# A two-layer hybrid decoder step: the opening of layer 0 rearranged (norm factors as rows, fewer and longer weight sums, waits by row group)

## The chip, the cores and the metric

The kernel runs on one core of one Trainium2 chip. The metric is the device time of one execution in microseconds: 2112.86 us, the median of three runs (2112.59 to 2115.5). The core has five engines that run side by side and wait for each other by semaphores: TensorE (PE in the profile) for matrix products and transposes, VectorE (DVE), ScalarE (ACT), GpSimd (POOL), and SyncE (SP), which only issues transfers. TensorE's clock has two levels, 1.2 and 2.4 GHz; the profile shows it as the granted clock, 0.50 or 1.00.

## The reference

Two layers work on a prompt of 2048 tokens and on a sample of 64 tokens (8 sequences of 8), with width 1024. Each layer does this:

```python
u = rms_norm(x, norm_gain)                  # x / rms(x) * gain, the gain has 1024 values
proj = u @ w_in                             # 1024 x 3592, in float32
# three head groups read the same proj
h_m = sigmoid(mo) * mlstm(mq, mk, mv, i_pre, f_pre, C0, n0, m0)
h_r = retention(rope(rq), rope(rk), rv, S0)
h_a = window_attention(aq, ak, av, k_buf, v_buf, pos0, sinks, rel_table)
mix = concat(head_norm(h_m) * silu(mz), head_norm(h_r) * silu(rz), h_a * silu(az))
x = x + mix @ w_out
```

A last RMSNorm follows. The states, the normalisers and the last window of keys and values are outputs as well. What matters here is the projection: the gain is multiplied into the rows of the weights, and the weights are used in a form that has to be made on the chip first.

## The kernel before

The prompt is processed in chunks of 128 tokens, 16 a layer. The projection's weights lie in eight blocks of columns; in the order in which they are made ready they are gates (264 columns), rqk, akv (256), rvz, aq, az, mqk, mvo (512 each where no number stands). A block has eight row groups of 128 rows, which is the contraction split into eight. A product of one chunk with one block is 24 matmuls, three a row group, because both operands are kept as two float16 parts: high by high, high by low, low by high (`pair_products`, L547 to L552).

In the first unit of each layer, a block goes through these steps:

1. *Load.* GpSimd issues the load of the block's float32 weights (`load_raw`, L398). The first three are issued at once, each later one when the maximum of an earlier block is known; the last waits for the low parts of the third block.
2. *Size.* ScalarE sums the absolute values of row groups 0 to 5, one sum a row group, by an activation with an accumulator (`abs_sum` L447, `block_sum` L455), alternating between two scratch rows, so that a sum waits only for the one before the previous. VectorE takes the absolute maximum of row groups 6 and 7, multiplies all eight numbers by the size of the gain, and takes the largest (`block_max`, L469 to L477).
3. *Maximum over partitions.* TensorE turns the column of 128 maxima into a row (`top_turn`, L504), VectorE reduces it to one number (`top_of_all`, L508), and TensorE spreads that to all partitions (`top_spread`, L512).
4. *Scale.* VectorE derives a power of two from it and the scales of the eight row groups (`block_scale`, L519 to L529).
5. *Parts.* ScalarE writes the high part, one instruction a row group (`block_hi`, L537), and VectorE the low part behind it (`block_lo`, L544).
6. *Products.* TensorE multiplies the first chunk with the block (`first_block`, L989), once all eight low parts are there, and the sample with the block (`sample_block`, L1002). ScalarE empties both (`evac_first` L1383, `evac_sample` L1406); SyncE stores the sample's result (`keep_sample`, L774), and ScalarE's copy of sample block p waits for the store of block p - 2.

The order of instructions on each engine is written out by hand: `start_act` and `start_dve` hold the opening, `prompt_pe`, `prompt_act` and `prompt_dve` the first unit, `prompt_sp` SyncE's part. Between the blocks stand other steps of the first unit: the copy and the store of a Toeplitz table of the attention bias (1600 KB, sent from 8 partitions, L717, `store_toeplitz`), read back by `load_bias` (L723 to L727); the gate rows (L1886 to L1908); GpSimd's rope (L2302 to L2311).

In the opening, SyncE issues, in this order, the first prompt rows, the identity, small constants, the norm factors (L379) and the sample's rows (L706). VectorE does the prompt's norm, the size of the gain (L467), all of the sample's norm (L1720 to L1729), then the gates block's maximum. ScalarE does the sample's root before the gates block's sums. After the first unit, a loop does the other chunks; there the weights are ready, and each block is one product of 24 matmuls.

Layer 1's blocks go through the same functions during the output projection of layer 0.

## Time and profile before

| | |
|---|---|
| time, median of 3 runs | 2112.86 us (2112.59 to 2115.5) |
| the profiled execution, its own time | 2116.62 us |
| its span in the profile | 2114.80 us |
| TensorE busy | 2016.7 us, 95% of the span |
| VectorE / ScalarE / GpSimd busy | 1661.0 / 890.0 / 330.4 us |
| mean granted clock of TensorE | 0.979 |

The profile is one execution, with times from the start of its span. A row of the timeline or of the groups names the line of the kernel, the engine, the operation, and what is written from what. In square brackets stands how long the engine had stood before it, and what ended that.

### The profile page before, as it was taken

Reading aid. Unit: us, or ns where it says so; the run is one execution under the profiler, and the core shown is the slowest. Engines: PE = TensorE matmul, PEld = TensorE weight load, DVE = VectorE, ACT = ScalarE, POOL = GpSimd, SP = SyncE. Lnnn points to the kernel's source line nnn. Section 1 sums busy time; section 2 is a strip of 40 time slices with the busy share of each in tenths; the row PEclk is TensorE's granted clock in tenths of the full one; section 3 lists DMA queues with packets and bytes.
Section 4 is the critical chain, followed back from the end, with each engine's and each line's share of the span. In section 5 each row is a group of like instructions: output and inputs, shape, how many; then the busy total and the mean of one; then the engine's idle time right before and its main releaser. Section 6 shows DMA issues by size and latency. Waiting matters only on the chain.

```text
span 2114.8 us, 36272 instructions
## 1 busy us (share of the span) xinstructions
PE 2016.7 (95%) x12814; PEld 1133.3 (54%) x12814; DVE 1661.0 (79%) x3966; ACT 890.0 (42%) x2334; POOL 330.4 (16%) x320
## 2 busy tenths in 40 slices
PE   3799999999999999999979999999999999998997
PEld 2465555555555555444455555555555555554453
DVE  5778887888888888675465888888888888887856
ACT  5854444445444445231255444444444444462100
POOL 1101121111111112120010111111111111111200
PEclk9899999999999999999989999999999999999999
DMA  7411121111121114785522111211111211257642
GB/s 247 125 40 42 42 50 43 51 41 41 41 61 41 41 42 131 173 248 155 185 105 64 42 42 42 61 42 41 41 41 44 50 41 51 63 157 177 160 119 90
DMA packets 258349, 175.09 MB, mean 83 GB/s; under 512 B 217880, under 2 KB 231897, under 8 KB 258077
## 3 DMA queue, kind: packets, MB, share of 16 engines
q1 hardware_dynamic: 242244, 142.14, 26.4%
q0 software_dynamic: 7424, 29.43, 3.9%
q10 hardware_dynamic: 8568, 2.18, 0.5%
q8 instruction: 52, 0.85, 0.2%
q14 instruction: 61, 0.49, 0.1%
HBM read 85.29 MB, written 42.29 MB: 60 GB/s over the span
## 4 chain that ended last, share of the span: by engine, by line
PE 62%; issue 18%; DVE 12%; POOL 3%; ACT 3%; DMA 2%; POOLq 0%; SPq 0%; DVEq 0%; ACTq 0%
PE J L551 35%; PE J L1263 12%; PE W L954 2%; DVE W L544 2%; PE W L965 1%; PE J L1002 1%; PE W L1038 1%; ACT junk L450 1%; DMA sc_xr<-in_x_sample 1%; POOL ST L2274 1%; PE W L1068 1%; PE W L1056 1%; PE W L1027 1%; POOL ge L2269 1%; POOL ST L2265 1%
## 5 line engine op out<-in xcount | busy, mean ns | idle before, releaser
L551 PE MATMUL J<-W,x_mix 128*128 128x512 f16 (+2 forms) x3072 | 612.6, 357 | 5.9 <-ACT PB L1383 3.9
L551 PE MATMUL J<-W,uT_mix 128*128 128x512 f16 (+2 forms) x3072 | 612.9, 357 | 2.7 <-DVE W L544 2.6
L551 PEld LDWEIGHTS J<-W,x_mix 128*128 128x128 f16 x3072 | 300.0, 99 | 278.9 <-issue 14.9
L551 PEld LDWEIGHTS J<-W,uT_mix 128*128 128x128 f16 x3072 | 299.7, 99 | 275.8 <-issue 13.9
L1383 ACT ACTIVATE PB<-J,out_scale 128x512 f32<-128x512 f32 (+2 forms) x256 | 154.3, 603 | 294.0 <-PE J L551 286.2
L1353 ACT ACTIVATE ST<-ST,small 128x1024 f16<-128x1024 f32 x32 | 36.7, 1148 | 198.6 <-DVE small L1844 198.6
L1263 PE MATMUL J<-W,EM_qkR_mix 128*128 128x512 f16 x480 | 115.3, 379 | 0.0
L2274 POOL TENSOR_TENSOR ST<-ST,ge 128x512 f32<-128x512 f32 x32 | 67.8, 2117 | 220.5 <-DVE ST L1828 220.5
L1263 PE MATMUL J<-W,x_mix 128*128 128x512 f16 x400 | 99.6, 389 | 0.0
L1263 PE MATMUL J<-W,uT_mix 128*128 128x512 f16 x400 | 99.4, 388 | 0.0
L1347 ACT ACTIVATE sc_xr<-sc_xr,small 128x128 f32<-128x128 f32 x256 | 98.6, 388 | 0.0
L1747 DVE TENSOR_TENSOR ge<-ge,gr 128x512 f32<-128x512 f32 (+1 forms) x96 | 57.4, 598 | 35.3 <-ACT gr L1319 35.3
L2269 POOL TENSOR_TENSOR ge<-ge,PB 128x512 f32<-128x512 f32 x32 | 40.6, 1270 | 272.7 <-DVE ge L1749 272.7
L2265 POOL TENSOR_TENSOR ST<-HH,ge 128x512 f32<-128x512 f32 x32 | 41.4, 1293 | 250.9 <-DVE HH L1784 250.9
L1263 PEld LDWEIGHTS J<-W,EM_qkR_mix 128*128 128x128 f16 x480 | 47.0, 98 | 55.6
L1819 DVE TENSOR_TENSOR ST<-ST,k 128x2048 f16<-128x2048 f16 x62 | 73.1, 1220 | 2.0 <-DMA ST<-ST 2.0
L954 PE MATMUL W<-kTA,qTA_part 64*128 64x256 f32 (+1 forms) x512 | 62.3, 382 | 9.2 <-DVE SR L1766 9.2
L1263 PEld LDWEIGHTS J<-W,x_mix 128*128 128x128 f16 x400 | 40.1, 100 | 48.6 <-issue 5.1
L1263 PEld LDWEIGHTS J<-W,uT_mix 128*128 128x128 f16 x400 | 40.0, 100 | 48.2 <-issue 4.7
L1623 ACT ACTIVATE small_o<-small_o 128x1 f32<-128x1 f32 (+1 forms) x17 | 3.4, 202 | 147.7 <-DVE small_o L2184 131.3
L2285 POOL TENSOR_TENSOR ge<-ge,PB 128x256 f32<-128x256 f32 x32 | 23.8, 743 | 254.9 <-DVE ge L1749 254.9
L1749 DVE SCALAR_TENSOR_TENSOR ge<-ge,gr 128x512 f32<-128x512 f32 (+1 forms) x96 | 59.8, 623 | 3.3
(467 smaller groups left out, 3523.9 us busy)
## 6 DMA issues: line engine op xcount, KB each, us to landing
W<-in_w_in POOLq DMA_DIRECT2D x8, 2048.0 KB, 12.3
mix_d<-ST SPq DMA_DIRECT2D x32, 512.0 KB, 2.6
sc_xr<-in_x_prompt SPq DMA_DIRECT2D x20, 512.0 KB, 4.1
sc_xr<-x SPq DMA_DIRECT2D x20, 512.0 KB, 3.8
ST<-in_w_in POOLq DMA_DIRECT2D x4, 2048.0 KB, 12.5
W<-in_w_out SPq DMA_DIRECT2D x4, 2048.0 KB, 8.3
PB<-in_x_prompt SPq DMA_DIRECT2D x6, 512.0 KB, 3.7
x<-PB SPq DMA_DIRECT2D x6, 512.0 KB, 3.6
```

Source lines behind the costliest of these rows:

```text
L544: nc.vector.scalar_tensor_tensor(pair[b][:, k, 1, :], raw(layer, b)[:, k, :], gs[:, j, k:k + 1], pair[b][:, k, 0, :], ALU.mult, ALU.subtra ...
L551: mm = nc.tensor.matmul(out, stationary(k, a), moving[:, k, b, :], start=(k == 0 and n == 0), stop=(k == KT - 1 and n == 2))
L954: mm = MM(bank[:, t * 256 + lo:t * 256 + 256], qTA[64 * kv:64 * kv + 64, t, :], kTA[64 * kv:64 * kv + 64, lo:256], start=True, stop=True)
L1263: mm = nc.tensor.matmul(J[n], of_tile[:, s, k, :], w[:, cols], start=(k == 0 and i == 0), stop=(k == KT - 1 and i == 2))
L1347: op = af(sc[:, h, :], sc[:, h, :], ACT.Exp, bias=mx[:, h:h + 1], accum_out=rs[:, h:h + 1])
L1383: return af(dst, src, ACT.Copy, scale=scale)
L1747: V.tensor_tensor(y, y, y0, ALU.mult).then_inc(E["gate_inverses"], 1)
L1749: V.scalar_tensor_tensor(y, y, 2.0, y0, ALU.subtract, ALU.mult, reverse0=True).then_inc(E["gate_inverses"], 1)
L1819: op = V.tensor_tensor(pT_both[s], pT_both[1], kept, ALU.mult)
L2265: G.tensor_tensor(mixmr, HH, ge[:, 256:768], ALU.mult).then_inc(E["mixmr_ready"], 1)
L2269: G.tensor_tensor(ge[:, 768:1280], ge[:, 768:1280], PB[:, AZ:IN_COLS], ALU.mult).then_inc(E["gates_a"], 1)
L2274: G.tensor_tensor(mixa, mixa, ge[:, 768:1280], ALU.mult).then_inc(E["mixa_ready"], 1)
```

## The change

- The norm factors are laid out as rows in memory: the array of one layer is 128 x 8 instead of 1024, so that each partition's eight factors lie together, and one plain load brings them.
- SyncE issues the sample's rows first, then the factors, then the small constants.
- The size of a block: in layer 0, ScalarE sums three row groups by one instruction, two sums a block (`abs_sum_wide`), each waiting for the one before; their scratch space is the attention bias, whose load therefore moves from after the fourth block to after the seventh and waits for all of layer 0's sums. VectorE takes one maximum over row groups 6 and 7 and multiplies the largest number by the largest factor of the partition (`gtop`) instead of each by its own. `block_max` is split; the part behind the sums is `block_top`.
- ScalarE does the gates block's sums before the sample's root. The sample's norm is split in three (`sample_size`, `sample_scale`, `sample_rows`), and VectorE does the gates block's maximum between the first two and its scale before the third.
- TensorE waits for the low parts row group by row group in the first unit's products. In layer 0, VectorE takes the maximum of the next block but one after two row groups of low parts for blocks 1 to 3, instead of after all eight.

```diff
         def load_gain(eng, layer):
-            eng.dma_start(norm_g[:], A["norm_gain"][layer].rearrange("(k p) -> p k", p=P),
-                          allow_slow_non_contiguous=True).then_inc(gain_loaded, 16)
+            eng.dma_start(norm_g[:], A["norm_gain"][layer]).then_inc(gain_loaded, 16)
...
+        def abs_sum_wide(act, out, rows):
+
+            wait(act, C["sum_ready"], sums[0])
+            unread = bias[:].rearrange("p h c -> p (h c)").bitcast(BF16)[:, 0:rows.shape[1] * rows.shape[2]]
+            nc.scalar.activation(unread.rearrange("p (k n) -> p k n", k=rows.shape[1]), rows, ACT.Abs, accum_out=out
+                                 ).then_inc(C["sum_ready"], 1)
+            sums[0] += 1
...
-            for k in range(SUM_KS):
-                abs_sum(act, wmax[:, j, k:k + 1], raw(layer, b)[:, k, :])
+            for i in range(SUM_GROUPS[layer]):
+                if layer == 0:
+                    abs_sum_wide(act, wmax[:, j, SUM_KS - 2 + i:SUM_KS - 1 + i], raw(layer, b)[:, 3 * i:3 * i + 3, :])
+                else:
+                    abs_sum(act, wmax[:, j, i:i + 1], raw(layer, b)[:, i, :])
...
             c_prep.step(V.scalar_tensor_tensor(gabs[:], norm_g[:], -1.0, norm_g[:], ALU.mult, ALU.max))
+            c_prep.step(V.tensor_reduce(gtop[:], gabs[:], AX.X, ALU.max))
...
-            st(V.tensor_reduce(wmax[:, j, SUM_KS:KT], raw(layer, b)[:, SUM_KS:KT, :], AX.X, ALU.max,
-                               apply_absolute_value=True))
-            dve.wait_ge(C["sum_ready"], LAYER_SUMS * layer + SUM_KS * (j + 1))
-            st(V.tensor_tensor(wmax[:, j, :], wmax[:, j, :], gabs[:], ALU.mult))
-            V.tensor_reduce(wtop[:, j:j + 1], wmax[:, j, :], AX.X, ALU.max).then_inc(C["max_ready"], 1)
+            st(V.tensor_reduce(wmax[:, j, SUM_KS:SUM_KS + 1], raw(layer, b)[:, SUM_KS:KT, :].rearrange("p k n -> p (k n)"),
+                               AX.X, ALU.max, apply_absolute_value=True))
+
+        def block_top(dve, layer, j):
+            V, st = nc.vector, c_prep.step
+            dve.wait_ge(C["sum_ready"], sums_before(layer, j + 1))
+            first = SUM_KS - SUM_GROUPS[layer]
+            st(V.tensor_reduce(wmax[:, j, SUM_KS + 1:KT], wmax[:, j, first:SUM_KS + 1], AX.X, ALU.max))
+            V.tensor_scalar(wtop[:, j:j + 1], wmax[:, j, SUM_KS + 1:KT], gtop[:], None, ALU.mult
+                            ).then_inc(C["max_ready"], 1)
...
             sp.dma_start(ident, A["c128"][:, 0:P]).then_inc(ident_loaded, 16)
+            sp.dma_start(xs, A["x_sample"].rearrange("b t d -> (b t) d")).then_inc(S["x"], 16)
+            load_gain(sp, 0)
             sp.dma_start(k4[:], A["c4"]).then_inc(ident_loaded, 16)
-            load_gain(sp, 0)
-            sp.dma_start(xs, A["x_sample"].rearrange("b t d -> (b t) d")).then_inc(S["x"], 16)
...
-                if layer == 0 and p == 3:
+                if layer == 0 and p == 6:
+                    sp.wait_ge(C["sum_ready"], sums_before(layer, NBLK))
                     load_bias(sp)
...
-                pe.wait_ge(C["lo"], KT * (NBLK * layer + p + 1))
-                pair_products(J[bank][:, 0:BLOCK[b][1] - BLOCK[b][0]], lambda k, s: uT[:, s, k, :], pair[b]
-                              ).then_inc(E["proj_done"], 1)
+                pair_products(J[bank][:, 0:BLOCK[b][1] - BLOCK[b][0]], lambda k, s: uT[:, s, k, :], pair[b],
+                              lambda k: pe.wait_ge(C["lo"], KT * (NBLK * layer + p) + k + 1)).then_inc(E["proj_done"], 1)
...
             prompt_rstd(act, 0)
+            block_sum(act, 0, 0)
             sample_rstd(act, 0)
-            block_sum(act, 0, 0)
             prompt_uT_hi(act, 0)
...
             gain_size(dve, 0)
-            sample_norm(dve, 0, xs)
+            sample_size(dve, 0, xs)
             block_max(dve, 0, 0)
+            block_top(dve, 0, 0)
             top_of_all(dve, 0, 0)
+            sample_scale(dve, 0, xs)
+            block_scale(dve, 0, 0)
+            sample_rows(dve, 0, xs)
             prompt_uT_lo(dve, 0)
-            block_scale(dve, 0, 0)
...
                 block_lo(dve, layer, 0)
+                block_max(dve, layer, 1)
+                block_top(dve, layer, 1)
                 sample_uT_lo()
-                block_max(dve, layer, 1)
                 top_of_all(dve, layer, 1)
                 block_scale(dve, layer, 1)
                 block_max(dve, layer, 2)
-                block_lo(dve, layer, 1)
+                block_top(dve, layer, 2)
+                block_lo(dve, layer, 1, range(0, 2))
                 top_of_all(dve, layer, 2)
+                block_lo(dve, layer, 1, range(2, KT))
                 block_scale(dve, layer, 2)
                 block_max(dve, layer, 3)
-                block_lo(dve, layer, 2)
+                block_top(dve, layer, 3)
+                block_lo(dve, layer, 2, range(0, 2))
                 top_of_all(dve, layer, 3)
+                block_lo(dve, layer, 2, range(2, KT))
+                block_scale(dve, layer, 3)
                 block_max(dve, layer, 4)
-                block_scale(dve, layer, 3)
-                block_lo(dve, layer, 3)
+                block_top(dve, layer, 4)
+                block_lo(dve, layer, 3, range(0, 2))
                 top_of_all(dve, layer, 4)
+                block_lo(dve, layer, 3, range(2, KT))
...
         if name == "norm_gain":
             a = np.ascontiguousarray(a.reshape(DEPTH, KT, P).transpose(0, 2, 1))
```

## Rows read from the trace of the kernel before

**Rows 1.** Busy time by stage: start:end, length, busy time and instructions of each engine, clock, DMA.
```profile
0.00:130.00 130.00, 84.56 (x705) 53.14 (x707) 80.39 (x217) 84.34 (x211) 14.09 (x19) 0.91 0.53 159
130.00:860.00 730.00, 727.25 (x4689) 420.48 (x4688) 620.58 (x1499) 340.74 (x886) 131.98 (x122) 1.00 0.21 51
```

**Rows 2.** Chain of waits: start, length, what the end waited for.
```profile
2.55 18.38 DMA sc_xr<-in_x_sample
```

**Rows 3.** Who waited for whom, first 30 us: total, times, longest.
```profile
DVE gabs L467 <- DMA norm_g<-in_norm_gain: 11.8, 1, 11.8
```

**Rows 4.** DMA issues, first 30 us: count, KB each, us from issue to landing.
```profile
W<-in_w_in POOLq DMA_DIRECT2D x1, 1056.0 KB, 8.7
...
norm_g<-in_norm_gain SPq DMA_DIRECT2D x1, 4.0 KB, 18.3
```

**Rows 5.** DMA queues, 9 to 10 us: packets, MB, share of 16 engines' time.
```profile
q0 software_dynamic: 90, 0.36, 97.9%
q1 hardware_dynamic: 90, 0.00, 5.9%
```

**Rows 6.** Timeline of the opening: start us, us, engine, line, operation.
```profile
1.29 1.93 POOL L398 DMA_DIRECT2D W<-in_w_in  x2 [0.84 <-POOLq L2971]
...
7.87 0.75 DVE L1704 TENSOR_SCALAR x_mix<-x_mix,small 128x1024 f32<-128x1024 f32 x1
...
23.00 0.20 ACT L1302 ACTIVATE small_n<-small_n 64x1 f32<-64x1 f32 x1 [15.94 <-DVE small_n L1724]
...
26.18 0.16 DVE L477 TENSOR_REDUCE wtop<-wmax 128x1 f32<-128x8 f32 x1
...
28.89 3.36 ACT L537 ACTIVATE W<-W,gs 128x264 f16<-128x264 f32 x8 [2.06 <-DVE gs L524]
```

**Rows 7.** Timeline, sums over one row group: 512 and 256 columns.
```profile
32.63 0.61 ACT L450 ACTIVATE junk<-W 128x512 bf16<-128x512 f32 x1
...
36.70 0.40 ACT L450 ACTIVATE junk<-ST 128x256 bf16<-128x256 f32 x1
```

**Rows 8.** Timeline, blocks 1 to 3.
```profile
39.31 5.01 ACT L537 ACTIVATE W<-W,gs 128x512 f16<-128x512 f32 x8 [0.16 <-DVE gs L524]
...
56.90 2.79 PE L551 MATMUL J<-W,uT_mix 128*128 128x256 f16 x24
...
57.72 5.01 ACT L537 ACTIVATE W<-W,gs 128x512 f16<-128x512 f32 x8 [0.54 <-DVE gs L524]
...
58.47 7.17 DVE L544 SCALAR_TENSOR_TENSOR W<-W,gs 128x512 f16<-128x512 f32 x8 [0.73 <-ACT W L537]
```

**Rows 9.** Timeline from block 3's sample on, then busy time by stage.
```profile
88.47 0.45 ACT L1406 ACTIVATE qTA_part<-J,out_scale 128x256 f32<-128x256 f32 x1
...
96.55 7.95 PE L551 MATMUL J<-W,uT_mix 128*128 128x512 f16 x24
...
96.50:102.00 5.50, 5.50 (x15) 2.01 (x16) 3.25 (x11) 4.77 (x14) 1.45 (x2) 0.52 0.12 27
102.00:112.00 10.00, 10.00 (x84) 5.92 (x83) 8.13 (x18) 7.95 (x14) 0.00 (x0) 1.00 0.22 64
```

**Rows 10.** Chain of waits, layer 0's first output product.
```profile
853.37 5.29 PE J L1263 x24
```

**Rows 11.** Timeline, the bias load's second part and the bias's first reader.
```profile
90.72 5.22 SPq L727 DMA_DIRECT2D bias_s<-toep  x8
...
138.36 0.69 DVE L1795 SCALAR_TENSOR_TENSOR sc_xr<-W,bias 128x512 f32<-128x512 f32 x1
```

**Rows 12.** Chain of waits, between the layers.
```profile
911.95 0.10 DVE gabs L467
```

**Rows 13.** The table's store, then line 774, the stores of sample block 1.
```profile
48.65 0.80 SPq L717 DMA_DIRECT2D toep<-ge  x1
...
L774 SPq DMA_DIRECT2D ps_d<-qTA_part x2: 1587/4064/6542, 57.2 to 58.8; - x2
...
DMA to landing us min/median/max: 9.6/18.5/27.4
```

**Rows 14.** DMA queues, 56 to 60 us.
```profile
q0 software_dynamic: 210, 0.83, 51.4%
q1 hardware_dynamic: 120, 0.19, 45.4%
```

More of the change, by code:

```diff
@@ L441, in build, with sums_before @@
         C = {n: sem("c_" + n) for n in ["sum_ready", "max_ready", "top_psum", "top_ready", "top_spread", "scale_ready", "hi", "lo"]}
[L442 removed]
+        c_prep = Chain("dve_prep", 2 + 4 * NBLK)
         SUM_KS, WO_SUMS = 6, 6
[L444 removed]
+        SUM_GROUPS = [2, SUM_KS]
         sums = [0]
+        def sums_before(layer, j):
+            return SUM_GROUPS[layer] * j + (SUM_GROUPS[0] * NBLK + 2 * WO_SUMS if layer else 0)
         def abs_sum(act, out, row):
@@ L545, in block_lo, with pair_products @@
                                                pair[b][:, k, 0, :], ALU.mult, ALU.subtract).then_inc(C["lo"], 1)
-        def pair_products(out, stationary, moving):
+        def pair_products(out, stationary, moving, before=None):
             for k in range(KT):
+                if before:
+                    before(k)
                 for n, (a, b) in enumerate(((0, 0), (0, 1), (1, 0))):
@@ L1711, in prompt_uT_lo, with sample_size @@
             op.then_inc(E["uT_ready"], 1)
+        ss, sa, sv, sy, sx = (small_n[:, a:b] for a, b in ((0, 12), (12, 14), (14, 15), (16, 17), (17, 18)))
         def sample_norm(dve, layer, rows):
+            sample_size(dve, layer, rows)
+            sample_scale(dve, layer, rows)
+            sample_rows(dve, layer, rows)
+        def sample_size(dve, layer, rows):
             V, st = nc.vector, dve_norm.step
-            ss, sa, sv, sy, sx = (small_n[:, a:b] for a, b in ((0, 12), (12, 14), (14, 15), (16, 17), (17, 18)))
             dve_norm.begin(dve, layer)
@@ L1724, in sample_norm, with sample_scale, sample_rows @@
             V.tensor_scalar(sv, sv, EPS, None, ALU.add).then_inc(raised("x_var"), 1)
+        def sample_scale(dve, layer, rows):
             dve.wait_ge(*seen("x_rstd", layer))
-            newton(V, st, sy, sv, sx)
+            newton(nc.vector, dve_norm.step, sy, sv, sx)
             dve_norm.end()
+        def sample_rows(dve, layer, rows):
             wait(dve, o_stored[2], 16 * layer * SLOT_TILES[2])
-            V.tensor_scalar(xs, rows, sy, None, ALU.mult).then_inc(raised("u"), 1)
+            nc.vector.tensor_scalar(xs, rows, sy, None, ALU.mult).then_inc(raised("u"), 1)
         def attention_dve(dve):
@@ L2006, in prompt_dve @@
                 block_max(dve, layer, 5)
+                block_top(dve, layer, 5)
                 rows_scan(n)
@@ L2017, in prompt_dve @@
                 block_max(dve, layer, 5)
+                block_top(dve, layer, 5)
                 rows_in(n)
@@ L2033, in prompt_dve @@
             block_max(dve, layer, 6)
+            block_top(dve, layer, 6)
             if layer == 0:
@@ L2039, in prompt_dve @@
             block_max(dve, layer, 7)
+            block_top(dve, layer, 7)
             block_scale(dve, layer, 6)
@@ L2210, in output_dve @@
                     block_max(dve, layer + 1, 0)
+                    block_top(dve, layer + 1, 0)
                 if at == 9:
@@ L2218, in output_dve @@
                     block_max(dve, layer + 1, 1)
+                    block_top(dve, layer + 1, 1)
                 if at == 15:
@@ L2227, in output_dve @@
                     block_max(dve, layer + 1, 2)
+                    block_top(dve, layer + 1, 2)
                 if at == 23:
@@ L2238, in output_dve @@
                     block_max(dve, layer + 1, 3)
+                    block_top(dve, layer + 1, 3)
                 if at == 32:
@@ L2241, in output_dve @@
                     block_max(dve, layer + 1, 4)
+                    block_top(dve, layer + 1, 4)
             if not last_layer:
@@ L2974 @@
         a = np.ascontiguousarray(inputs[name])
+        if name == "norm_gain":
+            a = np.ascontiguousarray(a.reshape(DEPTH, KT, P).transpose(0, 2, 1))
         arrays["in_" + name] = a
```

5 lines of the change are left out of this document (2 added, 3 removed).

## Prediction

> **What bounds the kernel now.** I read the stages first: to 130 us TensorE is busy 84.56 of 130.00 us, from 130 to 860 us 727.25 of 730.00 us [rows 1]. The second stage runs at TensorE's own pace, so what the first unit of layer 0 saves stays saved, provided no later stage waits for something that does not move with it. The chain of waits, read next, says what the opening consists of: 18.38 us of it are one transfer, the sample's rows [rows 2]. The waits name what is in front of it: VectorE stood 11.8 us for the norm factors [rows 3]. They were issued at 2.09 us and took 18.3 us to land, so 20.4, though they are 4 KB; the sample's rows, queued behind, landed at 2.55 + 18.4 = 20.95. The gates weights, issued at 1.29, took 8.7 us and lay ready at 10.0 [rows 4]. The queues show why: in one microsecond SyncE's queue moved 90 packets of next to no bytes, the weights' queue 90 packets and 0.36 MB [rows 5]. With 1024 single values, 1024 / 90 = 11.4 us go into the factors. After the opening the first unit is a chain on ScalarE and VectorE (sums, scale, high part, low part for each of eight blocks) in which TensorE mostly waits.
>
> The profiled execution took 2116.62 us (span 2114.80, so 1.82 around it), 3.76 more than the median 2112.86. I work out a difference on its timeline and subtract it from the median. A change under 0.2% (4.2 us) could not be told from none.
>
> **A: from the start to the gates' first high part (28.89 us).** Factors as rows are 128 packets in place of 1024: 1.4 us at that rate, an estimate from [rows 5]. The sample's rows now go in front; 0.26 MB at 0.36 MB/us are 0.7 us. Both follow the prompt's first rows, whose norm VectorE has ended at 7.87 + 0.75 = 8.62 [rows 6]; that norm is 4 us of steps, so the rows came by about 4.6, and 2.1 later is about 7 (estimate). Bounds: earlier than 8.6 is worth nothing; landing at 10.0 costs 0.5, as ScalarE's sums end late anyway.
> VectorE then: factors' size and their maximum, two small steps, 0.4; the sample's moments, from the landing at 20.95 to 23.00, 2.0; done at 11.0. Meanwhile ScalarE sums the gates: they land at 10.0 plus 0 to 0.7, as the sample's 0.26 MB are now served between them; I take 10.4. A sum over 512 columns takes 0.61 and one over 256 takes 0.40 [rows 7], so 0.82 ns a column and 0.19 fixed. The new one has 3 x 264 = 792 columns: 0.84, plus 0.19 because the next sum now waits until this one has delivered (an estimate: the fixed part once more): 1.03. Two give 2.1, so 12.5. The two small steps after it end at 12.9 (before: at 26.34). Before, the first high part began 2.55 later; there the low part of the prompt's transpose stood in front of the scale, now the last of the sample's norm (four small steps, 0.74) does, finished at 14.4; the scale takes 0.69. The high part begins at 15.1. **A saves 13.8.** Bounds 12.5 to 14.3.
>
> **B: from there to the second block's high part (28.89 to 39.31 [rows 8], 10.42).** After the 3.36 of block 0's high part VectorE does the sample's rows (0.74) and the low part of the transpose (1.26) before block 0's low part. That delays the low part by some 1.5 against its high part, but TensorE no longer waits for all of it: it follows row group by row group, after the sample's transposes, from about 18.3 to 22.6. ScalarE: high part to 18.4, sample's copy to 19.0, block 1's two sums. One is 0.19 + 1536 x 0.00082 + 0.19 = 1.64; two take 3.3 against six at 0.61 = 3.7; done at 22.3. Tops 22.7, the transposed maximum behind the first products at 23.0, the sample's low part 0.69 beside it, spread 24.1, scale, high part at 24.8. That is 9.7. **B saves 0.7** (0 to 1.5).
>
> **C: to the fourth block's high part (39.31 to 57.72, 18.41).** VectorE takes the maximum after two row groups, so TensorE starts block 1's product at about 28 and ends it at 35.5 even at the slow level (7.95 at most [rows 9]); the sample's follows to 38.3. ScalarE then never waits for TensorE: 5.0 high part, 0.3, sums 3.3, 0.5 table copy, 3.3 high part, sums 3.3, 0.7, 0.5 = 16.9, so the fourth high part begins at 41.7. **C saves 1.5** (0 to 2.0). Below: long sums could cost more a column than short ones; if they gain nothing, 0.8 goes here and 0.8 in E.
>
> **D: to the end of its low part (57.72 to 65.64, 7.92).** Here the new order gives back. Block 2's product waits for ScalarE to empty the bank (41.2) and, TensorE having stood 2.7 us, runs at the slow level; it took 2.79 fast [rows 8], so some 4.8. The maximum of block 4 stands behind it on TensorE, and VectorE now waits for it after two of eight row groups, the other six behind. It goes on at 46.6, six groups of 0.67 follow: 50.7, thus 9.0 after 41.7. Before, all eight took 7.17, slowed by GpSimd's rope beside them; now the wait lies over that. **D loses 1.1** (0 to 2.5; at the fast level it would gain 0.6).
>
> **E: the rest of the first unit.** The chain of rows, high part 4, masks and sums 6 has the same instructions; blocks 5 and 6 each have their sums on it, 0.4 saved each; block 7's lie beside TensorE, busy from 96.55 [rows 9]. The waits by row group bring nothing from block 4 on: each product stands behind the spread of the next maximum, which VectorE raises after all eight. **E saves 0.8** (0 to 1.0).
>
> **F: costs elsewhere.** Eight waits a block cost TensorE nothing: the output product that waits by row group takes 5.29 for 24 matmuls [rows 10], the time of any product at the fast level. The bias load moves behind the sample's seventh block and waits for all layer 0 sums: from 90 to about 101 on the new timeline. SyncE's issues for it take 5.8 (0.6 and 5.22), which is over at 107, before SyncE's next store at 110, and the first reader comes at 138.36 - 15 = 123 [rows 11]. If its 16 us of room were gone, each microsecond late would count. Layer 1 keeps its six sums; the moved maximum has as many steps as before. The maximum of the factors stands once in front of VectorE's part of the chain at 911.95 [rows 12]: **costs 0.2.** Layer 1's factor load lies beside products.
>
> **Sum:** 13.8 + 0.7 + 1.5 - 1.1 + 0.8 - 0.2 = 15.5. 2112.86 - 15.5 = 2097.4.
>
> **Rivals.** (1) *The table's store becomes the wait.* It goes out at 48.65; the sample's block 1 is stored behind it and lands at 58.8 + 27.4 = 86.2; ScalarE's copy of sample block 3 needs that and came at 88.47 [rows 9, 13], 2.3 to spare. The issue moves by 14.7 (the table copy stands ahead of D and E), the reader by 15.8: 1.2 to spare. If the store takes 4 longer than before, as it now begins beside more weight loads, ScalarE waits 2.8: 2100.2. For it: the queue used 45% of the engines' time while the weights' queue had 51% [rows 14]; against: before, too, the last part of one weight load and two whole ones lay beside it. The Trainium skill, DMA: Bandwidth & Descriptors, section Why a DMA increments its semaphore by 16 and not by 1, limits a transfer whose slowest dimension is 8 to 8 engines; the 45% agree. By that the store cannot use what is freed and keeps its length: the forecast stands with its 1.2.
> (2) *Weights come late.* The fourth block's load now goes out at 13.2, into SyncE's constants; three loads (4.1 MB) and this one (2.1 MB) at 0.36 MB/us are 17.2 us from 4.6, and with the prompt's constants, some 1.3 MB with the sample's rows, 21: it lands at about 26 to 28, needed at 30.2. Were it 5 later than 28, C would lose 2.8: 2100.2. For it: the opening pulls the same bytes 15 us earlier; against: each later load has more room than this one.
> (3) *The factors stay slow,* as if the row form brought nothing: VectorE starts again at 20.4, tops at about 23.9 instead of 26.34, so 2.4, and B to E 1.9: 2108.6. Against: the packet counts.
> (4) *Slower: TensorE stays at its slow level.* Starting blocks on their first row group leaves it with holes. At 96.5 the granted clock was 0.52, at 102 to 112 1.00 [rows 9]. If it stayed at 1.2 GHz from block 5 to the end of the first unit, some 32 us of products would take about 20 more (part of it idle): 2112.86 - 15.5 + 20 = 2117. It decides from where the level does not return by block 6. Against: from block 5 on order and waits are as before. The Trainium skill, TensorE: Matmul & The Clock Gate, section HAM oscillation — how this bites in real kernels, tells of a kernel in which a wait before every group of products put the array back to its slow level each time. [Rows 9] show that for block 5 already in the kernel before.
>
> **Chances.** Forecast 0.70 with 2095.5 to 2099.5; (1) 0.10, (2) 0.08, (3) 0.03, (4) 0.03; 0.06 for a loss not listed, 2101 to 2106. Range: the bounds add up to 19.2 saved on one side (14.3 + 1.5 + 2.0 + 0.6 + 1.0 - 0.2) and 9.8 on the other (12.5 + 0 + 0 - 2.5 + 0 - 0.2); both together are unlikely, so 2094.5 to 2102.5, which holds (1) and (2). Faster 0.95, same 0.02, slower 0.03.
>
> **What would show it.** VectorE's step on the factors right after 8.62 and not at 20.43; the first high part at 15.1; block 1's product beginning beside its low part; a VectorE wait of about 2 us for the transposed maximum of block 4; sums of 1.45 in pairs; ScalarE's fourth sample copy at 72.7 with no wait; TensorE without gap from 81 instead of 96.55. Wrong if the first high part comes after 17, or if a wait on a transfer stands in front of ScalarE between 30 and 80.

## The result, and the profile after

| | before | after |
|---|---|---|
| median of the timed runs | 2113.18 us (2112.59 to 2117.34, 5 runs) | 2087.75 us (2086.40 to 2092.07, 5 runs) |
| profiled execution | 2116.62 us, span 2114.8 | 2087.75 us, span 2085.9 |

The ratio is 0.9879 (95% interval 0.9864 to 0.9894): 25.4 us saved where 15.5 were forecast (2097.4, range 2094.5 to 2102.5). It is faster, as forecast, but ends below the range. In the profiled executions the spans differ by 28.9: the profiled execution of the kernel before took 3.4 us more than the median of the timed runs, so the parts that the two traces show add up to about 28 and not to 25.4.

A unit is the work on one chunk; a loop runs over twelve of a layer's sixteen chunks, two units a pass, so six passes with five jumps back. I compared the two traces at one ScalarE instruction that comes once in each unit (line 1353 before, 1376 after). The time saved up to it is 16.1 us in layer 0's second unit and 15.95 through the whole of layer 0's loop, 15.1 just behind it (908.34 against 893.23), 17.4 at the head of layer 1's loop (1294.68 against 1277.34) and 29.7 at its end (1738.69 against 1708.95). The four marks of layer 1's loop, the kernel before first:

```profile
1294.68 1.15 ACT L1353 ACTIVATE ST<-ST,small 128x1024 f16<-128x1024 f32 x1 [6.40 <-DVE small L1844]
1738.69 1.15 ACT L1353 ACTIVATE ST<-ST,small 128x1024 f16<-128x1024 f32 x1 [6.47 <-DVE small L1844]
```
```profile
1277.34 1.15 ACT L1376 ACTIVATE ST<-ST,small 128x1024 f16<-128x1024 f32 x1 [6.41 <-DVE small L1880]
1708.95 1.15 ACT L1376 ACTIVATE ST<-ST,small 128x1024 f16<-128x1024 f32 x1 [6.48 <-DVE small L1880]
```

So the opening brought what the sum said, and **12.4 us came from the loop of layer 1**, which the change hardly touches.

The busy time by stage of the kernel before, in layer 1's loop (columns as in [rows 1]), which the prediction did not read:

```profile
1180.00:1400.00 220.00, 217.43 (x1427) 127.34 (x1426) 182.31 (x443) 97.31 (x249) 39.72 (x38) 1.00 0.18 44
1400.00:1600.00 200.00, 194.41 (x1260) 113.21 (x1260) 165.58 (x402) 87.04 (x229) 33.58 (x32) 1.00 0.17 44
1600.00:1800.00 200.00, 197.36 (x1270) 113.78 (x1267) 168.78 (x409) 87.48 (x231) 34.38 (x33) 1.00 0.18 46
```

The same of the kernel after, with the rows that answer [rows 1] first:

```profile
0.00:114.00 114.00, 80.24 (x703) 52.67 (x704) 80.19 (x218) 79.14 (x147) 14.55 (x19) 0.94 0.58 181
114.00:844.00 730.00, 727.14 (x4683) 420.83 (x4684) 619.91 (x1499) 340.20 (x885) 131.98 (x122) 1.00 0.21 51
1164.00:1384.00 220.00, 220.00 (x1451) 129.41 (x1450) 185.65 (x453) 96.78 (x247) 40.73 (x38) 1.00 0.18 45
1384.00:1584.00 200.00, 200.00 (x1281) 115.03 (x1279) 170.25 (x417) 91.72 (x249) 35.81 (x33) 1.00 0.17 43
1584.00:1784.00 200.00, 200.00 (x1285) 115.50 (x1283) 168.58 (x416) 92.34 (x243) 34.47 (x32) 1.00 0.18 46
```

Before, TensorE was idle for 10.8 of these 620 us; after, for none. The chain of waits of the kernel before shows the place, at the start of a pass of the loop (start, length, what the end waited for; "issue" is time in which nothing that the profile shows was waited for; L695 is the loop's own line, DVEq VectorE's sequencer):

```profile
1396.06 2.73 issue
1398.80 0.05 DVEq L695
...
1398.90 0.04 DVEq L1755
...
1398.98 0.29 DVE kTA L1756
1399.27 1.89 issue
1401.17 0.43 DVE HH L1762
```

VectorE jumps back, stands 2.7 us, goes through three instructions (the loop's first on line 695, one on a register, the copy of line 1756) and stands 1.9 us again. Then the queues that carry instructions. Queue 14 (packets, MB, share) in layer 1's loop, 1290 to 1770 us, first of the kernel before, then of the kernel after:

```profile
q14 instruction: 25, 0.20, 0.1%
```
```profile
q14 instruction: 1, 0.01, 0.0%
```

25 packets are five in each of the five jumps back, 8 KB apiece. Layer 0's loop of the kernel before, with the same 328 VectorE instructions a pass, had 3 in all between 250 and 740 us. That queue 14 carries VectorE's code is shown below, where instructions added on VectorE alone move its packets. That gave the first theory.

The opening of the kernel after (timeline: start us, us, engine, line, operation), to be read against [rows 6, 8, 9]:

```profile
11.49 0.86 ACT L462 ACTIVATE bias<-W 128x792 bf16<-128x792 f32 x1 [4.46 <-DMA W<-in_w_in]
12.04 0.17 DVE L482 SCALAR_TENSOR_TENSOR gabs<-norm_g 128x8 f32<-128x8 f32 x1 [3.45 <-DMA norm_g<-in_norm_gain]
12.30 1.97 PE L950 MATMUL T<-k,x_mix 128*128 128x128 f32 x8 [12.30 <-DMA k<-const_c]
...
17.62 3.35 ACT L558 ACTIVATE W<-W,gs 128x264 f16<-128x264 f32 x8 [1.81 <-DVE gs L545]
...
27.25 5.01 ACT L558 ACTIVATE W<-W,gs 128x512 f16<-128x512 f32 x8 [0.35 <-DVE gs L545]
...
30.17 5.35 PE L574 MATMUL J<-W,uT_mix 128*128 128x512 f16 x24
...
43.06 1.32 ACT L558 ACTIVATE W<-W,gs 128x512 f16<-128x512 f32 x2
...
47.10 0.28 DVE L529 TENSOR_REDUCE top_one<-W 1x1 f32<-1x128 f32 x1 [1.09 <-PE W L525]
47.31 4.86 DVE L565 SCALAR_TENSOR_TENSOR W<-W,gs 128x512 f16<-128x512 f32 x6
...
73.66 0.46 ACT L1429 ACTIVATE qTA_part<-J,out_scale 128x256 f32<-128x256 f32 x1
...
81.57 5.35 PE L574 MATMUL J<-W,uT_mix 128*128 128x512 f16 x24
```

The issues of its first 30 us, to be read against [rows 4]:

```profile
W<-in_w_in POOLq DMA_DIRECT2D x1, 1056.0 KB, 10.2
...
sc_xr<-in_x_sample SPq DMA_DIRECT2D x1, 256.0 KB, 8.8
...
norm_g<-in_norm_gain SPq DMA_DIRECT2D x1, 4.0 KB, 9.7
```

### The profile page after: what moved, and what is told of

Read it like the earlier page. It is cut to its first block, busy times and chain, and to the rows that moved or that the text cites. A ratio compares the mean times of both kernels' runs of the same rounds, so it can differ in the third digit from the quotient of the medians.

```text
span 2085.9 us, 36212 instructions
## 1 busy us (share of the span) xinstructions
PE 2007.0 (96%) x12814; PEld 1130.9 (54%) x12814; DVE 1659.3 (80%) x3968; ACT 885.3 (42%) x2270; POOL 333.8 (16%) x320
## 4 chain that ended last, share of the span: by engine, by line
PE 85%; DVE 8%; ACT 3%; DMA 2%; issue 1%; SPq 0%; POOL 0%; DVEq 0%; ACTq 0%
PE J L574 53%; PE J L1286 12%; PE W L978 3%; PE W L989 2%; PE W L1061 1%; PE W L1091 1%; ACT W L558 1%; PE W L1079 1%; PE W L1050 1%; DVE W L565 1%; PE T L1070 1%; PE W L964 1%; DMA ST<-ST 1%; PE J L1025 1%; PE W L996 1%
## 5 line engine op out<-in xcount | busy, mean ns | idle before, releaser
L1783 DVE TENSOR_TENSOR ge<-ge,gr 128x512 f32<-128x512 f32 (+1 forms) x96 | 57.3, 597 | 35.3 <-ACT gr L1342 35.3
```

Of the source, the lines that this page charges most:

```text
L1783: V.tensor_tensor(y, y, y0, ALU.mult).then_inc(E["gate_inverses"], 1)
```

## The experiments

**Three more instructions in the kernel before** (on VectorE, while it waits for the first rows anyway):

```diff
             clear_states(dve)
+            for i in range(3):
+                V.memset(pad[0:1, i:i + 1], 0.0)
             prompt_norm(dve, 0)
```

> The kernel before with three more memsets of one element at VectorE's start, where it waits for the first rows anyway. Theory 1 (place of the code): the loop of layer 1 is fetched anew in each pass, five fetches of 8 KB a pass, because its 328 VectorE instructions lie across one page of 8 KB too many; three instructions further on, as in the changed kernel, they fit. Then the 25 extra fetches go, the loop's passes take 96 us instead of 98.5 to 99, about 12 us in all, and the opening stays as it was (first high part at 28.9): about 2101 us. Theory 2 (the time saved in layer 1's loop comes from the earlier start, from other phases or from transfers that meet differently): nothing changes, 2113.

Measured: 2106.86 us beside 2117.26 for the kernel before on the same chip, ratio 0.9954 (0.9940 to 0.9967), 10 us faster (7 to 13). The 2101 expected counted from 2113; on this chip the same 12 us would have been 2105. In the trace the distance to the kernel before grows from 1.3 us at the head of layer 1's loop to 13.7 at its end: the whole 12.4. No instruction packet falls between 1290 and 1770 us, and TensorE has no idle time left (busy time by stage):

```profile
1184.00:1384.00 200.00, 200.00 (x1304) 116.64 (x1302) 169.70 (x422) 90.57 (x236) 36.17 (x34) 1.00 0.18 44
1384.00:1584.00 200.00, 200.00 (x1290) 115.41 (x1289) 169.31 (x409) 88.79 (x231) 36.88 (x33) 1.00 0.19 46
```

Theory 2 falls: nothing but three memsets was added, and the opening was even 0.8 us later (first high part at 29.71), layer 0's loop 1.9. The 12.4 is a figure of the traces; the timed runs alone bear out 10.

**Forty more in the changed kernel** (the same edit with 40):

> The changed kernel with forty more memsets of one element at VectorE's start, behind its own and ahead of its wait for the first rows. Theory 1: by the place that layer 0's loop must have in its page (about 29 of 128 instructions, if layer 1's starts at 0 to 2), forty more put it past 56, and its 328 instructions lie across four pages instead of three: now layer 0's loop pays five times 2.4 us, 12 us, with five fetches a pass, and layer 1's loop (40 to 42) still pays nothing: 2100 us. Theory 2: at most the memsets' own time, under 0.5 us: 2088.

Measured: 2092.89 us, ratio 0.9885 (0.9870 to 0.9900), 4 to 5 us behind the changed kernel (2087.75 and 2089.02 in its two sets of runs), where 12 were expected. Against the kernel before, the intervals of the three ratios overlap (0.9885, 0.9879 and 0.9863), so the loss is shown by the trace and not by the times. The packets came as said, 27 between 250 and 740 us, in layer 0's loop:

```profile
q14 instruction: 27, 0.22, 0.1%
```

But they cost 3.0 us in the five passes, 0.6 each, not 2.4. The timeline shows one stand of VectorE at the jump and none behind it:

```profile
352.28 0.42 DVE L1788 SCALAR_TENSOR_TENSOR ge<-ge,gr 128x256 f32<-128x256 f32 x1
355.33 0.29 DVE L1795 COPY kTA<-W 128x128 f32<-128x128 f32 x1 [2.63 <-PE W L966]
355.54 0.41 DVE L1801 TENSOR_TENSOR HH<-W,k 128x256 f32<-128x256 f32 x1
```

(The profile puts the 2.63 down to TensorE; without fetches the same wait is 2.19 in the kernel after.) So the expected price was wrong, and the number of fetches did not give it.

**97 more in the changed kernel**, to put layer 0's loop where layer 1's had been:

> The changed kernel with 97 more memsets of one element at VectorE's start. The trace of the kernel before shows VectorE, after the jump back in layer 1's loop, go through three instructions and then stand again for the second fetch: the loop begins three instructions ahead of a page's end, at 125 of 128. From this every loop's place follows; with 40 more, layer 0's loop began at 68 and had five fetches a pass, but lost 0.6 us a pass and not the 2.5 of layer 1's loop in the kernel before. Refined theory: the first fetch, at the jump, lies largely beside TensorE's product; the second is what costs, and it is waited for only when few instructions of the loop stand ahead of the page's end. With 97 more, layer 0's loop begins at 28 + 97 = 125 as layer 1's did before: it loses 2.5 us a pass, 12 in all; layer 1's begins at 97, has 31 instructions ahead of the page's end, and loses 0.6 a pass, 3 in all: 2103 us. Rival (layer 0's loop has more slack than layer 1's, whatever the place): 0.6 a pass in it, 3 in all, and 3 to 12 in layer 1's: 2094 to 2103, with layer 0's passes at 96.5 us.

Measured: 2106.81 us, ratio 0.9953 (0.9936 to 0.9970), 17.8 behind the changed kernel in the same set of runs (2089.02), where 15 were expected. Layer 0's loop lost 16.0 us, 3.2 a pass (the marks of two passes stand at 502.64 and 601.84, 99.2 apart instead of 95.9), layer 1's 3.3, 0.7 a pass. At each of layer 0's five jumps VectorE now stands 4.8 to 5.1 us in one piece before the loop's third instruction, about the 2.7 and the 1.9 together:

```profile
459.55 0.29 DVE L1795 COPY kTA<-W 128x128 f32<-128x128 f32 x1 [4.84 <-issue]
```

and TensorE is idle for 10.4 of 490 us there and for 2 of 480 in layer 1's loop:

```profile
250.00:740.00 490.00, 479.58 (x3072) 278.15 (x3071) 402.22 (x974) 214.40 (x565) 84.27 (x80) 0.99 0.18 45
1290.00:1770.00 480.00, 478.05 (x3079) 276.39 (x3077) 404.80 (x989) 216.50 (x570) 84.44 (x80) 1.00 0.18 45
```

The rival (layer 0's loop has more slack) falls, and the refined theory holds at these two places, with 3.2 and 0.7 a pass for 2.5 and 0.6. That the copy comes behind both stands here, while it came between them before, says that layer 0's loop began at 126 and not at 125: its place in the changed kernel is 29, one more than I had counted. Where that one instruction comes from is not known.

**Where the edge lies: 16, 20, 24, 28 and 29 more in the changed kernel**, single runs:

> The changed kernel with 28 more memsets at VectorE's start. By the counted places layer 0's loop begins at 28 + 28 = 56, and its 328 instructions end with the third page (56 + 328 = 384 = 3 x 128). If what decides is whether the loop fits into three pages, there is no extra fetch, and layer 0's passes stay at 95.9 us.

> The same with 29: the loop begins at 57 and its last instruction, the jump, lies in a fourth page. If the theory's edge is right, each of layer 0's passes now has five fetches, and loses 0.6 us; layer 1's loop has none. If the edge lies elsewhere (between 29 and 68), nothing changes against 28.

> The changed kernel with 16 more memsets at VectorE's start: layer 0's loop begins at 44 and ends 12 instructions ahead of its third page's end. With 28 more it ended right at the page's end and was fetched anew in every pass, against what was expected; layer 1's loop beginning at 40 was not. If the next page is called for some ten or more instructions before the loop's last one, the edge lies between 40 and 56. Here either: with five fetches a pass and passes of 97.4 us if the edge is under 44, with none and 95.9 if it is above.

> The same with 20: the loop begins at 48 and ends 8 instructions ahead of the page's end. None and 95.9 us a pass if the edge is above 48.

> The same with 24: the loop begins at 52 and ends 4 instructions ahead of the page's end. None and 95.9 us a pass if the engine calls for the next page only when it is within 4 instructions of it.

Measured, with the places put right by one; 40 and 97, with the medians of their runs, stand beside the single ones:

| more | start in its page | end of the loop (third page ends at 384) | q14 packets, 250 to 740 us | VectorE's stand at the jump, us | layer 0's loop lost, us | time, us |
|---|---|---|---|---|---|---|
| 16 | 45 | 373 | 1 | 2.2 | 0 | 2089.76 |
| 20 | 49 | 377 | 2 | 2.2 | 0 | 2089.12 |
| 24 | 53 | 381 | 2 | 2.2 | 0 | 2087.24 |
| 28 | 57 | 385 | 26 | 3.9 | 8.2 | 2095.34 |
| 29 | 58 | 386 | 26 | 3.3 to 3.5 | 5.8 | 2094.81 |
| 40 | 69 | 397 | 27 | 2.6 to 2.9 | 3.0 | 2092.89 |
| 97 | 126 | 454 | 26 | 4.8 to 5.1 | 16.0 | 2106.81 |

Single times say little here (four runs of the changed kernel lie between 2085.87 and 2091.10); packets, stands and losses are of the traces.

28 missed its expectation, by the one instruction if the place is right: with the start at 57 the jump lies in a fourth page. 29 cost twice the 0.6 a pass that was expected. The edge is between 53 and 57, where 384 - 328 = 56 puts it. At 28 VectorE stands 3.92 us at the jump:

```profile
455.54 0.29 DVE L1795 COPY kTA<-W 128x128 f32<-128x128 f32 x1 [3.92 <-issue]
```

The stand gives the price that the number of fetches doesn't. Without fetches VectorE stands 2.2 us there for TensorE, and a pass loses about what comes on top: 1.7 at 57 (measured 1.6), 1.2 at 58 (1.2), 0.5 at 69 (0.6), 2.7 at 126 (3.2), and in layer 1's loop of the kernel before, with its two stands of 2.6 and 1.9, 2.3 (2.5). Why the stand is longer at 57 and 58 than at 69 stays open. 71 and 70 instructions of the loop lie ahead of the page's end there, and 59 at 69, so the refined theory (the price falls with the instructions ahead of the page's end) does not cover them.

The Trainium skill, Runtime: NRT & Kernel Launch, section Instruction fetch mechanics, tells of this: most engines' instruction memory is 32 KiB, filled in order, and a taken jump to a target that is not in it has to wait for a fetch. The runs fit that size (three pages of the loop and, as I read it, one fetched ahead are four of 8 KB); none of them measures it by itself. The block of 16 KiB that the skill names doesn't agree for this engine: its packets are of 8 KB (25 packets, 0.20 MB), and the edge lies where pages of 128 instructions put it.

**The changed kernel again, and the opening taken apart.** First the kernel as it is:

> The changed kernel itself, with an empty line more at its end, as the measure for the other runs beside it: 2088 us by its own first runs, or 0.988 of the kernel before, with both loops free of extra fetches.

Measured: 2089.02 us, ratio 0.9863 (0.9843 to 0.9883). Its trace is a measure of what differs between two executions of one program: 15.2 saved in layer 0's loop instead of 15.95, and 15.7 instead of 17.4 at the head of layer 1's. The traces of all runs give a wider one. From the last unit of layer 0's loop to the head of layer 1's the code is that of the changed kernel in its two traces and in eleven of its variants (all but the one in which TensorE waits for all low parts), and this stretch of about 496 us takes between 492.9 and 498.8 (498.3 in the kernel before). So a difference of a few microseconds at the end of the first unit need not be there any more at the head of layer 1's loop, nor in the time.

The layout of the norm factors alone in the kernel before:

```diff
-            eng.dma_start(norm_g[:], A["norm_gain"][layer].rearrange("(k p) -> p k", p=P),
-                          allow_slow_non_contiguous=True).then_inc(gain_loaded, 16)
+            eng.dma_start(norm_g[:], A["norm_gain"][layer]).then_inc(gain_loaded, 16)
```

> The kernel before with the norm factors laid out as rows and nothing else changed (its VectorE has as many instructions, so layer 1's loop pays as before). If the layout alone carries the opening, the sample's rows land at about 11 instead of 20.95, the sums follow as before, and the first high part begins at about 19 instead of 28.89: 10 us faster, 0.9953 of the kernel before. If the other edits are needed for it (order of the sums and the norm), it is at most 6 us.

Measured: 2106.55 us, ratio 0.9945 (0.9928 to 0.9963), 10.7 us. First high part at 20.18 instead of 28.89, 9.6 saved through layer 0's loop, and layer 1's loop pays as before (24 packets). Of the 15.2 to 15.95 the layout brings 9.6, the other edits about 6. The expectation of 10 us was met in the sum; the rows landed at 12.3, not 11.

The factors and the small constants ahead of the sample's rows:

```diff
+            load_gain(sp, 0)
+            sp.dma_start(k4[:], A["c4"]).then_inc(ident_loaded, 16)
             sp.dma_start(xs, A["x_sample"].rearrange("b t d -> (b t) d")).then_inc(S["x"], 16)
-            load_gain(sp, 0)
-            sp.dma_start(k4[:], A["c4"]).then_inc(ident_loaded, 16)
```

> The changed kernel with the norm factors and the small constants issued ahead of the sample's rows instead of behind them. If the rows' 0.26 MB held up the small transfers behind them, the factors land at about 7 instead of 12.0, VectorE's step on them comes right behind the prompt's norm at 8.6, TensorE's prompt transposes start at 8.7 instead of 12.3, the rows land at 11, and the first high part begins at about 16.5 instead of 17.6: 2086.5 us. If each small transfer takes 9 us once the weights are on the way, whatever is ahead of it, nothing changes: 2087.8.

Measured: 2087.91 us, ratio 0.9856 (0.9840 to 0.9872). The factors land 3.6 us after their issue instead of 9.7, the rows 7.6 instead of 8.8, TensorE's transposes start at 8.73 and the first high part at 15.58:

```profile
sc_xr<-in_x_sample SPq DMA_DIRECT2D x1, 256.0 KB, 7.6
norm_g<-in_norm_gain SPq DMA_DIRECT2D x1, 4.0 KB, 3.6
```

Layer 0's loop runs 2.0 us earlier than in the first trace of the changed kernel, 2.7 than in the second. At the head of layer 1's loop the gain is gone against the first (17.40 and 17.34 saved) and 1.8 against the second, and the times show none (2087.91 beside 2087.75 and 2089.02).

Six sums again in layer 0:

```diff
-        SUM_GROUPS = [2, SUM_KS]
+        SUM_GROUPS = [SUM_KS, SUM_KS]
...
-                if layer == 0:
-                    abs_sum_wide(act, wmax[:, j, SUM_KS - 2 + i:SUM_KS - 1 + i], raw(layer, b)[:, 3 * i:3 * i + 3, :])
-                else:
+                if True:
                     abs_sum(act, wmax[:, j, i:i + 1], raw(layer, b)[:, i, :])
```

> The changed kernel with six sums of one row group in layer 0, as before, instead of two over three groups. Theory: the two wide sums save 0.45 us a block where they stand on the chain, in blocks 1, 2, 3, 5 and 6, and nothing in block 0, whose sums end at 13.4 while the maximum is wanted at 15.0: 2.2 us slower than the changed kernel, 2090 us. Rival (the sums are hidden by the other steps of the new order): 2088.

Measured: 2090.61 us, ratio 0.9879 (0.9864 to 0.9894). In the trace it is 60.2 us from the first high part to the sixth, against 57.3 and 57.5 in the two traces of the changed kernel: 2.7 to 2.9 more, some 0.7 in each of the four blocks whose sums were named, where 0.45 was expected. With block 5's product slower too (7.98 us against 5.35 and 7.04) layer 0's loop is 3.65 and 2.9 later. At the head of layer 1's loop nothing of it is left (17.7 saved, against 17.3 and 15.6), and the timed runs alone would not tell this from none.

TensorE waits for all eight low parts again:

```diff
-                              lambda k: pe.wait_ge(C["lo"], KT * (NBLK * layer + p) + k + 1)).then_inc(E["proj_done"], 1)
+                              lambda k: pe.wait_ge(C["lo"], KT * (NBLK * layer + p + 1))).then_inc(E["proj_done"], 1)
```

> The changed kernel in which TensorE waits for all eight low parts of a block before its product, as before, instead of one row group after the other. Block 0's product starts at 22.7 instead of 20.6, so the maximum of block 1 behind it is 1.5 to 2 us late; block 1's starts at 33.8 instead of 30.2, and the maximum of block 3 behind it and the sample's product comes at 42 instead of 36.4. The fourth high part starts 3 to 5 us later than at 43.1, and the end of the first unit with it: 2092. If ScalarE is the bound there and not TensorE: 2089.

Measured: 2094.36 us, ratio 0.9913 (0.9890 to 0.9936). From the first high part to the second it takes 11.6 us, against 9.6 and 9.4; the fourth comes at 49.05, against 43.06 and 43.24; layer 0's loop is 5.4 and 4.6 later than in the two traces of the changed kernel. At the head of layer 1's loop 1.9 and 0.2 of it are left. The ratio says slower (0.9913 beside 0.9863 for the changed kernel, intervals apart), though not beside its first set (0.9879, up to 0.9894). Block 1's product starts 5.8 late, behind the low parts, and runs mostly at the slow level (granted clock 0.69):

```profile
35.99 7.64 PE L574 MATMUL J<-W,uT_mix 128*128 128x512 f16 x24 [3.60 <-DVE W L565]
```

Against 30.17 and 5.35: the waits by row group save the start and, in this product, the level.

The maximum after all eight low parts in blocks 1 to 3 (shown for block 1):

```diff
-                block_lo(dve, layer, 1, range(0, 2))
+                block_lo(dve, layer, 1)
                 top_of_all(dve, layer, 2)
-                block_lo(dve, layer, 1, range(2, KT))
```

> The changed kernel in which VectorE takes the maxima of blocks 2, 3 and 4 after all eight low parts of the block before, instead of after two. The product of block 1 starts at 34.2 instead of 30.2, so the fourth high part is later by up to 3 us; in the next block the wait of 1.09 us for TensorE's maximum goes. 1 to 3 us slower than the changed kernel at the end of the first unit, 2090; if the early maximum brought nothing, 1 us faster, 2087.

Measured: 2090.36 us, ratio 0.9891 (0.9871 to 0.9912). The fourth high part comes at 45.53, 2.3 later than in the second trace of the changed kernel, and the next part gives 2 of it back (0.25 later in layer 0's loop, 1.0 later than in the first trace): expected was 1 to 3 in all. Taken early, the maximum brings at most 1 us in the traces, and the times don't tell it from none.

A last try at a better kernel joined the factors and small constants ahead of the rows with the maximum of block 4 taken after five low parts instead of two:

```diff
-                block_lo(dve, layer, 3, range(0, 2))
+                block_lo(dve, layer, 3, range(0, 5))
                 top_of_all(dve, layer, 4)
-                block_lo(dve, layer, 3, range(2, KT))
+                block_lo(dve, layer, 3, range(5, KT))
```

> The changed kernel with two small edits: the norm factors and the small constants issued ahead of the sample's rows (that alone began layer 0's loop 1.9 us earlier in its trace), and the maximum of block 4 taken after five low parts of block 3 instead of two, where VectorE waited 1.09 us for TensorE. Together 3 us earlier at the end of the first unit of layer 0. If this stays, 2085 us; if, as with the first of the two alone, the first unit of layer 1 takes it back, 2088.

Measured: 2086.97 us, ratio 0.9855 (0.9836 to 0.9875), beside 0.9863 for the changed kernel: not told apart. In its trace the first high part came at 16.40, 1.65 earlier than in the second trace of the changed kernel, and layer 0's loop 0.5 earlier (0.3 later than in the first); the 3 us expected there did not come. Block 5's product took 7.91, against 7.04.

## Why the prediction was wrong

**The step that failed** is the first, and with it F. "The second stage runs at TensorE's own pace, so what the first unit saves stays saved" was read from [rows 1], which end at 860 us, and F priced the edits elsewhere at 0.2. Nothing was said of layer 1's loop, so what it would gain stood at nothing. It did not run at TensorE's pace: 10.8 of 620 us idle there, and passes of 98.2 us (1345.89 to 1444.08) against 95.9 in layer 0's. "The moved maximum has as many steps as before" is near the point and misses it: not the steps' time counted, but that three more instructions stand ahead of the loop. The traces put **12.4 us** there, and three memsets in the kernel before bring the same 12.4. It was within reach of the trace: at each of the five jumps back a stand of 2.7 us, three instructions, a stand of 1.9 and five packets of code say that the loop begins three instructions ahead of a page's end, and the diff moves it by three. Priced at five times 98.2 - 95.9, 11.5 us, the forecast would have been about 2086.

The other half of that step, that what the first unit saves stays saved, is only true to within a few microseconds: see the 492.9 to 498.8 above.

**The opening** was right in its sum, 15.5 against 15.2 and 15.95 in the two traces, and less so in its parts. That the sum came out is in part luck: A fell 2.5 short, and C and E brought 2.8 more than forecast.

- A: 13.8 forecast, 11.3 measured, under its lower bound of 12.5. The mis-sized term is the landing of the sample's rows and the factors. I had them at about 7 and the gates' weights at 10.4; they came at 10.5, 12.0 and 11.5. I gave the sample's rows all the bandwidth (0.26 MB at 0.36 MB/us); they took 8.8 us beside the weights, and what is queued behind them waited too. With the factors ahead of them the first high part came at 15.58, half a microsecond from my 15.1. So A's steps on the engines were about right, and the order of the loads was not as good as I took it for. Nor had I seen that the small constants behind the rows hold TensorE's first transposes to 12.30. In the second trace A is 10.8. The first high part at 17.62 is also past the 17 that the prediction had set as a sign of being wrong; the sum held all the same, by what C and E brought.
- B: 0.7 forecast, 0.8 measured. A wide sum of 792 columns took 0.86, as forecast at 0.84.
- C: 1.5 forecast, 2.6 measured (18.41 against 15.81). Block 1's product started at 30.17, not 28, but at the fast level; the bound was 2.0. The run without waits by row group shows both parts of it.
- D: a loss of 1.1 forecast, 1.2 measured, the wait of 1.09 for the maximum of block 4 where it was said to be. In the second trace it is 1.7, with block 2's product at 5.30 us instead of 4.09 (the prediction had it at 4.8).
- E: 0.8 forecast, 2.5 measured (64.00 from the end of block 3's low part to layer 0's next unit, against 61.54), over its bound of 1.0. Block 5's product took 5.35 in this trace where [rows 9] have 7.95; in the second trace of the same kernel it took 7.04, and E is 2.4 there too (61.60):

```profile
82.24 7.04 PE L574 MATMUL J<-W,uT_mix 128*128 128x512 f16 x24
```

  Two runs with this product at the pace of the kernel before split it. With six sums (7.98 us) the stretch takes 63.95, as before; with 16 memsets and the wide sums (7.93 us) 62.69. By these about 1.25 of E are the wide sums, worth more than the 0.8 forecast, and 1.15 the faster product. TensorE had stood 3.79 us ahead of it in the kernel before, 2.92 and 3.23 in the two traces of the changed one. In the 14 traces of the changed kernel and its variants it took 5.35 us five times, about 7 five times and about 8 four times, and only with 8 is the stretch longer by 1 us or more; so that part of E does not come in every execution. And TensorE did not run without a gap from 81 us on, as the prediction says: it stood another 1.57 us ahead of block 6's product.
- F: the loop apart, the time saved moves from 15.95 to 15.1 and then to 17.4 at the head of layer 1's loop, and in the second trace from 15.2 to 16.6 to 15.7. One piece of this is the level (granted clock 1.00 in the first trace, 0.50 in the second): one product of 24 matmuls, shown here in the first and the second trace of the changed kernel. In the kernel before it took 5.44. The rest was not taken apart.

```profile
1054.21 2.86 PE L574 MATMUL J<-W,x_mix 128*128 128x264 f16 x24 [2.02 <-issue]
```
```profile
1053.24 5.44 PE L574 MATMUL J<-W,x_mix 128*128 128x264 f16 x24 [2.02 <-issue]
```

**The rivals.** (1) The table's store did not become the wait: ScalarE's copy came at 73.66 without waiting. (2) The weights were in time. (3) The factors did not stay slow, but 2.5 of the 13.8 was lost to a milder form of it. (4) TensorE did not stay at its slow level. Each rival was about the opening; none was about the rest of the kernel, so the range of 8 us left out the loop that made the difference.

## What to carry to other kernels

Before the sum is made, hold each loop's passes against each other: two loops with the same instructions whose passes differ (98.2 and 95.9 us here) have a cost that the code doesn't show, and a change elsewhere can take it away or bring it. For a loop of many instructions count where it begins: any instruction added or removed ahead of it shifts it, and here 3 of them were worth 12.4 us in the trace (10 in the timed runs), and 97 of them cost 17.8. When an edit changes the time by more than its own parts explain, pad the old kernel to the new one's instruction count before crediting the edit.

## What the runs showed of the hardware

- VectorE's instructions come in packets of 8 KB. A loop of 328 instructions had no fetches of its own at any of the places tried from 0 to 53 of a page of 128, and five a pass at 57, 58, 69, 97, 125 and 126 (places by the count of the program and the stands of the traces). The stand at the jump was 2.7 us in the kernel before, with a second one of 1.9 behind it, and 3.9 at 57.
- The same five fetches a pass cost this kernel between 0.6 and 3.2 us, by the place: about the length of VectorE's stand at the jump, less the 2.2 us that it stands there for TensorE in any case.
- A load of 4 KB behind one of 256 KB on the same queue, with weights under way on another, landed 9.7 us after its issue; ahead of it 3.6.
- Two executions of one program had the same product at 2.86 and 5.44 us after the same wait of 2.02 us. The granted clock was 1.00 in the one and 0.50 in the other. A microsecond or two in a stage where TensorE has gaps says nothing about an edit, unless the clock is read beside it.
